# First block's sparse attention: DVE and ACT work in single-head pieces, the first decay level ahead of the scores, and a projection tile inside the last step

## What is computed

```python
# 1. sparse attention (NSA): 8 heads, 2 kinds of keys (selected, sliding), on top of compressed keys
p_slc = softmax(where(causal, q @ k_sel.T, NEG)); o_slc = p_slc @ v_sel
p_win = softmax(where(win_ok, q @ k_win.T, NEG)); o_win = p_win @ v_win
o     = g0 * o_cmp + g1 * o_slc + g2 * o_win
y_a   = o @ w_proj_nsa
# 2. gated linear attention (GLA): attn[t, s] = sum_d q[t,d] k[s,d] exp(b[t,d] - b[s,d]), s <= t
o     = attn @ v;  o = rms_norm(o) * g * silu(r)
y_b   = o @ w_proj_gla
# mixed = sigmoid(m_a) * y_a + sigmoid(m_b) * y_b;  h = h + mixed @ w_out
# 3. the second block's modulations, for both of its layers
mod   = silu(c) @ ada_w[l] + ada_b[l]
```

## Time and profile before

| | us |
|---|---|
| median of 3 runs (range) | 1208.77 (1208.45 to 1209.26) |
| the profiled execution | 1204.53 |
| its span in the profile | 1202.7 |
| the stage: first scores to the first projection | 137.80 to 216.45 of the span |
| PE busy over the span | 1088.9 (91%) |
| DVE, ACT, POOL busy | 470.7, 411.8, 206.4 |

### The profile page before, as it was taken

How to read it: one execution, slowest core, us unless ns; L and a number is a source line. 1 busy time by engine, 2 the same in 40 slices (tenths; PEclk the granted TensorE clock), 3 DMA queues, 4 the chain that set the end, 5 groups by cost and what they waited for, 6 DMA issues and landing times. The chain is left out here.

```text
span 1202.7 us, 17403 instructions
## 1 busy us (share of the span) xinstructions
PE 1088.9 (91%) x6862; PEld 706.4 (59%) x6862; DVE 470.7 (39%) x1037; ACT 411.8 (34%) x786; POOL 206.4 (17%) x277
## 2 busy tenths in 40 slices
PE   8999888899898889788989899979999899999997
PEld 7887555557432324344545235346887676999775
DVE  4565366445200000133332112107747546344654
ACT  5444353343101001014332102004436454444872
POOL 1005363000000000002120000004422223001550
PEclk9999899999999999999999999999999999999998
DMA  9657399745799999999999999995531203766300
GB/s 364 233 173 259 126 350 351 266 175 226 286 425 426 422 426 415 424 427 401 418 428 422 422 423 421 424 419 205 172 128 53 89 21 121 223 182 190 107 20 35
DMA packets 55720, 333.58 MB, mean 277 GB/s; under 512 B 5840, under 2 KB 6096, under 8 KB 43216
## 3 DMA queue, kind: packets, MB, share of 16 engines
q1 hardware_dynamic: 55632, 332.39, 71.1%
HBM read 331.32 MB, written 1.05 MB: 276 GB/s over the span
## 5 line engine op out<-in xcount | busy, mean ns | idle before, releaser
L486 ACT ACTIVATE ab<-w 128x1024 fp32r<-128x1024 f32 (+2 forms) x117 | 122.0, 1049 | 178.9 <-PE ps L502 170.2
L496 DVE TENSOR_TENSOR ab<-w,ab 128x1024 fp32r<-128x1024 f32 (+2 forms) x96 | 116.8, 1223 | 133.4 <-ACT ab L486 133.0
L2548 PE MATMUL ps<-w,vT 128*32 128x512 f32 x1024 | 129.1, 629 | 41.2 <-DMA w<-in_w_gate 28.2
L502 PE MATMUL ps<-ab,uA 128*128 128x512 f32 x320 | 102.5, 402 | 5.8 <-POOL ab L496 2.6
L2548 PEld LDWEIGHTS ps<-w,vT 128*32 128x32 f32 x1024 | 29.1, 111 | 121.8 <-issue 79.7
L502 PE MATMUL ps<-UA,ab 128*128 128x256 f32 x512 | 93.8, 284 | 2.8 <-ACT h L1573 1.5
L502 PE MATMUL ps<-ab,UA 128*128 128x512 f32 (+1 forms) x288 | 87.9, 386 | 0.6 <-POOL UB L624 0.6
L502 PEld LDWEIGHTS ps<-UA,ab 128*128 128x128 f32 x512 | 80.2, 192 | 3.5 <-issue 1.7
L2596 PE MATMUL ps<-w,bT 128*32 128x512 f32 x512 | 62.0, 608 | 16.5 <-DMA w<-in_w_down 10.9
L502 PEld LDWEIGHTS ps<-ab,uA 128*128 128x128 f32 x320 | 60.5, 192 | 20.8 <-issue 3.4
L496 POOL TENSOR_TENSOR ab<-w,ab 128x1024 fp32r<-128x1024 f32 (+1 forms) x21 | 49.9, 2380 | 132.7 <-DVE Am L1804 88.1
(11 more groups left out here) (547 smaller groups left out, 1858.7 us busy)
## 6 DMA issues: line engine op xcount, KB each, us to landing
w<-in_w_gate SPq DMA_DIRECT2D x32, 2048.0 KB, 13.3
w<-in_w_up SPq DMA_DIRECT2D x32, 2048.0 KB, 12.9
w<-in_w_down SPq DMA_DIRECT2D x32, 2048.0 KB, 13.2
w<-in_w_ada SPq DMA_DIRECT2D x48, 512.0 KB, 7.6
w<-in_w_c SPq DMA_DIRECT2D x42, 512.0 KB, 4.5
w<-in_w_m SPq DMA_DIRECT2D x16, 512.0 KB, 5.3
w<-in_ab_out_w SPq DMA_DIRECT2D x10, 512.0 KB, 4.4
w<-in_w_out SPq DMA_DIRECT2D x8, 512.0 KB, 9.8
```

What stands on the lines that cost most here:

```text
L486: e.activation(sp.a(j), w.v, ACT.Copy).then_inc(sp.whole, 1)
L496: e.tensor_tensor(sp.b(j), w.v, sp.a(j).bitcast(F32), ALU.subtract).then_inc(sp.parts[j % NAB], 1)
L502: ins = e.matmul(out_, l[x], r[y], start=start and n == 0, stop=stop and n == 2)
L2548: ins = e.matmul(t.ps[o, :], ve[:, p % 2, 2 * c + k, o], w.v[:, 2 * a + k, :], start=c + k == 0, stop=c + k == 4)
```

## The change

**1. Single-head pieces.** `masked`, `weighted` (DVE), `turned`, `weights` (ACT) now do one head per call, and the table places the two heads in slots of their own. In the same table `turned_out` goes from slot 8 to 6, `weighted` from slot 5 to 7 and 9, and POOL's `roots` from slot 0 to 2.

**2. First decay level ahead.** `DECAY_AHEAD = 3`: each engine takes three steps of its decay generator before the stage. For POOL these hold level 0's L1073, L1074 and L1083, L1084 (lines 1074, 1075, 1084, 1085 now); for ACT level 0's exponential, behind the second L1659 copy and before the output of `m01`; for PE and DVE nothing but the yields. So all later decay work is written six slots earlier against the attention and the modulations.

**3. A projection tile in the last step.** PE's table gets `(1, 2, behind)`, which for the last pair calls `project`: `pnsa0` of row tile 0 is computed between the last pair's `turn` and `out`, in a bank of `FIVE`, after the copies of the row tile 0 pairs alone. Row tile 1 follows in its old place.

```diff
+        DECAY_AHEAD = 3
...
-            return nsa_steps([(0, 2, turn), (0, 0, scores), (5, 2, out)])
+            def behind(p):
+                if p == len(NSA_PAIRS) - 1:
+                    last()
+
+            return nsa_steps([(0, 2, turn), (0, 0, scores), (1, 2, behind), (5, 2, out)])
...
-            return nsa_steps([(2, 0, masked), (5, 1, weighted), (8, 2, turned_out)])
+            return nsa_steps([(1, 0, lambda p: masked(p, 0)), (2, 0, lambda p: masked(p, 1)), (6, 2, turned_out),
+                              (7, 1, lambda p: weighted(p, 0)), (9, 1, lambda p: weighted(p, 1))])
...
-            return nsa_steps([(1, 2, turned), (3, 0, weights)])
+            return nsa_steps([(1, 2, lambda p: turned(p, 0)), (2, 2, lambda p: turned(p, 1)),
+                              (3, 0, lambda p: weights(p, 0)), (6, 0, lambda p: weights(p, 1))])
...
-            return nsa_steps([(0, 1, roots)])
+            return nsa_steps([(2, 1, roots)])
...
+            def project(n, x, p, c, i, ring=ALL):
+                ts, t = slice(i * 128, (i + 1) * 128), bank.take(ring, p + str(c))
+                free(e, t)
+                if c == 0:
+                    for y in bank[n] if n == "ogT" else bank[n][i::2]:
+                        e.wait_ge(y.evac, y.n)
+                for k in range(4):
...
+                    ins = e.matmul(t.ps[:, :], x[:, k, ts], w.v[:, k % 2, :], start=k == 0, stop=k == 3)
+                ins.then_inc(t.full, 1)
...
+            decayed = pe_decayed(e, TWO)
+            for _ in range(DECAY_AHEAD):
+                next(decayed)
+            rest = turns(pe_modulations(e, ONE), decayed)
+            beside(pe_nsa(e, FIVE, lambda: project("nsa_o", ynT, "pnsa", 0, 0, FIVE)), rest)
...
+            decayed = act_decayed(e)
+            for _ in range(DECAY_AHEAD):
+                next(decayed)
             act_lin(e, S1, "m01", [xsm[:, i, 0, :] for i in range(2)], more=0, scaled=True)
-            rest = turns(act_modulations(e), act_decayed(e))
+            rest = turns(act_modulations(e), decayed)
```

More of the change, by code:

```diff
@@ L1218, in nsa_steps, with pe_nsa @@
                     yield
-        def pe_nsa(e, ring):
+        def pe_nsa(e, ring, last):
             turned = {}
@@ L1298, in turned_out, with turned @@
                 e.tensor_copy(ynT[:, j, i * 128:(i + 1) * 128], t.ps[:, 0:128]).then_inc(t.evac, 1)
-            return nsa_steps([(2, 0, masked), (5, 1, weighted), (8, 2, turned_out)])
+            return nsa_steps([(1, 0, lambda p: masked(p, 0)), (2, 0, lambda p: masked(p, 1)), (6, 2, turned_out),
+                              (7, 1, lambda p: weighted(p, 0)), (9, 1, lambda p: weighted(p, 1))])
         def act_nsa(e):
-            def turned(p):
+            def turned(p, hp):
                 n = 256 * (NSA_PAIRS[p][1] + 1)
[L1305 to L1311, removed]
@@ L1313, in weights @@
-            def weights(p):
+                u, t = 2 * p + hp, bank["nsa_t"][2 * p + hp]
+                if u >= 3:
+                    g = bank["nsa_o"][(u - 3) // 2]
+                    e.wait_ge(g.full, g.n)
+                e.wait_ge(t.full, t.n)
+                e.activation(bT[:, u % 3, 0:n], t.ps[:, 0:n], ACT.Copy).then_inc(t.evac, 1)
+            def weights(p, hp):
                 i, m = NSA_PAIRS[p][1], st[:, p % 4, :]
                 n = 128 * (i + 1)
[L1316 to L1325, removed]
@@ L1327, in act_nsa @@
-            return nsa_steps([(1, 2, turned), (3, 0, weights)])
+                u, t = 2 * p + hp, bank["nsa_s"][2 * p + hp]
+                e.wait_ge(t.evac, t.n)
+                if u >= 4:
+                    g = bank["nsa_t"][u - 4]
+                    e.wait_ge(g.full, g.n)
+                for kind in range(2):
+                    o, c = slice(kind * n, kind * n + n), 2 * hp + kind
+                    ins = e.activation(NSA_P[u % 4][:, o], bS[:, hp, o], ACT.Exp, bias=m[:, c:c + 1], scale=-1.0, accum_out=m[:, 4 + c:5 + c])
@@ L1543, in pe_first @@
                     for i in range(2):
-                        ts, t = slice(i * 128, (i + 1) * 128), bank.take(ALL, p + str(c))
-                        free(e, t)
-                        if i == 0 and c == 0:
-                            for y in bank[n]:
-                                e.wait_ge(y.evac, y.n)
-                        for k in range(4):
-                            w = W[f"{p}{c}.{k // 2}"]
-                            if i == 0 and k % 2 == 0:
-                                e.wait_ge(w.full, w.n)
-                            ins = e.matmul(t.ps[:, :], x[:, k, ts], w.v[:, k % 2, :], start=k == 0, stop=k == 3)
-                        ins.then_inc(t.full, 1)
-                    for k in range(2):
-                        W.release(f"{p}{c}.{k}", t.full, t.n)
+                        if c + i > 0 or n == "ogT":
+                            project(n, x, p, c, i)
             pe_idle_next(e, ALL, 4)
@@ L1856, in dve_first @@
             dve_lin(e, S1, "m01", more=0)
-            rest = turns(dve_modulations(e), dve_decayed(e))
+            decayed = dve_decayed(e)
+            for _ in range(DECAY_AHEAD):
+                next(decayed)
+            rest = turns(dve_modulations(e), decayed)
             beside(dve_nsa(e), rest)
@@ L1926, in pool_first @@
                 e.tensor_tensor(st[:, 2 + i, :], st[:, 2 + i, :], gate[:, i, 0:24:3], ALU.mult).then_inc(c_rec, 1)
-            beside(pool_nsa(e), turns(idle_modulations(), pool_decayed(e)))
+            decayed = pool_decayed(e)
+            for _ in range(DECAY_AHEAD):
+                next(decayed)
+            beside(pool_nsa(e), turns(idle_modulations(), decayed))
             pool_rsqrt(e, 2, 2, (squared, 2))
```

41 lines of the change are left out of this document (22 added, 19 removed).

## The result

| | before | after |
|---|---|---|
| median (range), 22 runs each | 1209.42 (1204.26 to 1218.50) | 1214.45 (1209.92 to 1221.67) |
| ratio | | 1.0039, 95% interval 1.0024 to 1.0054 |
| the profiled execution, its span | 1204.53, 1202.7 | 1214.65, 1212.8 |
| first scores to the last transposes (L570) | 85.59 | 92.47 |
| PE busy / not busy in it | 72.44 / 13.15 | 77.07 / 15.40 |

What follows compares the result with a forecast made beforehand. PE's own work was taken to set the stage, leaving only its waits to win. Start -4.9, middle 0, end +5.8, behind +0.3, clock +3.2 sum to +4.4 us: 1213.2 us, 8 in 10 from 1205.5 to 1216.5.

Steps and rivals of the forecast that it cites:

- start: Start of the stage, up to pair 1's scores: 4.9 us less, 1.5 of them the clock.
- middle, waits: Pair 1's scores to `out` of pair 5: PE's waits 5.85 us against 5.89 before, so no change.
- (a): End of the stage: chunk 11 waits 2.8 us for DVE, which has other work ahead of chunk 10's sum.
- (d): Last `turn` (pair 7), head 0: waits 1.35 us while DVE copies pair 6 out, sums chunk 11 and scales.
- (e): Last `turn`, head 1: waits 3.05 us, its scaling standing behind the GLA's four closing products on DVE.
- clock behind them: Lower PE clock after the end's long waits: +3.2 us, chunk 11 losing 1.5 and project tile 0 1.7.
- behind it: After the stage: `pgla0`'s second tile waits for bank 4, shared with tile 0; +0.3 us.
- (c): End of the stage: `out` of pair 6 waits 0.6 us for `bT`, 0.46 before.
- That the middle's waits go: Rival, faster: smaller pieces make the middle's 5.9 us of waits vanish, 1204.1 us; chance 0.22.
- The loads: Rival, slower still: modulation loads set the middle's pace, costing 2.4 us there, 1215.6 us; chance 0.08.
- The clock's rival: Rival, no change: the clock holds without any drop, sum +1.2 us, 1210.0 us; chance 0.22.
- The shift: Rival, no change: something behind the stage is late anyway and the 4.4 us vanish there; chance 0.06.

Runs made afterwards that it cites:

- ahead: Part 2 alone against the kernel before: first decay level ahead, old table of whole pairs, no projection tile in the last step; 1207.00 us, ratio 0.9981.
- scale: The change, with DVE scaling the last pair's head 1 directly behind head 0, ahead of the closing products; 1208.81 us, ratio 1.0006 to the kernel before.
- idle: The change, with 4 idle matmuls ahead of chunk 11's products and 5 between the last turn's heads; 1209.58 us, ratio 1.0011 to the kernel before.
- project: Part 3 alone against the kernel before: projection tile in the last step, old table, no decay level ahead; 1208.21 us, ratio 0.9991.
- ahead_project: Parts 2 and 3 against the kernel before, on the old table of whole pairs; 1207.19 us, ratio 0.9974.
- pieces: Part 1 alone against the kernel before: new table by head, no decay level ahead, no projection tile in the last step; 1213.23 us, ratio 1.0037.
- sums: The change, with DVE's closing chain of the GLA (copy, squares, closing products) written behind all modulations; 1214.82 us, ratio 1.0049 to the kernel before.
- ahead_project_sums: Parts 2 and 3 on the old table, with DVE's closing chain written behind all modulations; 1213.91 us, ratio 1.0033 to the kernel before.
- both: The change with the edits of `scale` and `sums` together; 1213.03 us, ratio 1.0031 to the kernel before.

## Why the prediction was right, point by point

**Direction and size.** 1213.2 was forecast, +4.4 us on the median; measured 1214.45, +4.7 by the ratio. The terms, read in the profiled executions:

| step | forecast | profile | also shown by |
|---|---|---|---|
| start | -4.9 | -5.10 | `ahead`, all with part 2: 6.14 to 6.15 us |
| middle, waits | 0 (5.85 for 5.89) | +0.8 (6.65) | |
| middle, clock | 0 | +1.6 | not in `scale`, `idle` |
| end (a), chunk 11 | 2.8 | 2.47 | `scale`, `idle` |
| end (d), (e), last `turn` | 1.35, 3.05 | 1.37, 2.70 | `scale` removes (e) |
| end, waits in all | +5.8 (9.1 for 3.36) | 8.31 - 3.36 = +4.95 | |
| clock behind them | +3.2 (1.5 and 1.7) | +4.4 (1.6 and 2.7) | `idle`: about 3.4 |
| behind it | +0.3 | +0.4 (7.51 for 7.10) | `project` |

Within the table: the middle's waits were mis-sized at level 4 (0.67 for 0.1), level 7 (1.02 for 0.6) and chunk 6 (0.53 for 0.8); level 3's 1.52 for 1.5 and chunk 2's 1.29 for 1.25 held. The end's larger waits were a little shorter than worked out, (c) too (0.46 for 0.6). Tile 0 took 5.91 us for 5.2, and head 1's transposes ahead of it 1.09 for 0.66. Some sums are looser than they look: the pieces named for level 3 give 1.3 us and not 1.5, those for (a) of the end 2.7 and not 2.8.

The signs that were named came: pair 1's scores 6.14 us after the first at a grant of 1.00, the waits of DVE's sum and scaling in their places, tile 0 near half its rate, and 53.71 busy us in the middle, under the 55 that would have spoken against it. Only the end of the stage came later than named: it is 6.9 us longer in the profile, where the terms gave 4.1.

**Where it was luck.** That the sum comes within half a microsecond of the median is partly luck. In the profiled execution the same terms come to 7.3 us (6.88 and 0.4), and two of them were off by about 0.8 with opposite signs: the middle's waits too low, the end's too high. The 0 for the middle hides two effects of 3.0 and -2.0 us (see `scale`): the level ahead adds waits, and the pieces take part of them away. The working counted them together and gave neither a size.

**The term that was wrong** is the clock in the middle. The forecast took the lower grant to follow waits of about 3 us, and put none behind level 3's 1.5 us. In this execution it followed that wait too and cost 1.83 - 1.16 + 2.87 - 1.92 = 1.6 us. It followed this wait in three of eight profiled executions (below), so the median should hold less of it than this profile.

**The rivals.** That the middle's waits go was wrong: 6.65 us are left. The breaking-up advice behind that rival (the Trainium skill, "Perfetto Trace Analysis", section "Optimizing Scalar/DVE Operations") says only that it may help, and here it does so in one place: beside the level ahead, the pieces shorten PE's waits in the middle from 8.47 to 6.65 us (`ahead_project` and `scale`). On the whole they lose: `pieces` alone is 1.0037, since a piece that is written later in its engine's queue is late for a PE that was never waiting for it. The loads did not bind: PE's timeline of the stage has no wait for a load, and `scale` took the middle in 58.74 us with loads at 355 GB/s, while the experts' stretch again moved 422 GB/s, above the 358 GB/s that the Trainium skill, "DMA: Bandwidth & Descriptors", section "Where 436 GB/s comes from", gives for a core. The clock's rival was wrong in its size: idle work takes some 3.4 us back. The shift was not swallowed.

**What the forecast did not say** is which parts (e) comes from. It needs two parts: with the pieces alone the closing products are written six slots later and start behind head 1's scaling (217.50 and 215.63 in that kernel's trace), and with parts 2 and 3 both scalings, in slot 5, stand ahead of them (208.53 and 209.05, the products from 211.32 on). Only six slots earlier and by head do the products slip between the two heads. (The two parts without the third were not run; the third changes nothing in DVE's queue.) This is the interaction spoken of above, and `scale`, which undoes it alone, gets 4 us back.

**Still open.** Whether (a) can be removed without a new wait: `sums` only showed that moving the whole closing chain is wrong. A finer order, with chunk 10's sum ahead of the copy and square alone, was not tried.

## What to carry to other kernels

Before moving work earlier or in smaller pieces, write out the queue of each engine around the waits that matter. A piece is worth something only if somebody waits for it: here the pieces took some 2 us of waits out of the middle, and the piece that was not early enough at the end (a scaling behind four products, a sum behind a copy and a square) made PE wait. Parts that are good one by one must be tried together with the table that places them; here two of three parts gained 0.26% together and the third lost more than that. Where a wait can't be removed, idle matmuls that fit into it cost nothing that could be measured here and may keep the clock for what comes behind: worth a try where such waits precede long products.

## What the runs showed of the hardware

A wait of the same length in the same place is followed by the lower clock in one execution and not in another. Behind the wait of 1.52 to 1.58 us ahead of level 3, level and chunk took 4.7 us in the change, in `ahead` and in `ahead_project_sums`, and 3.1 us (1.16 and 1.92) in `scale`, `sums`, `both`, `idle` and `ahead_project`. Behind 2.47 us chunk 11 took 3.55 us in the change, and behind 2.48 us 1.92 in `scale`. In `pieces` a wait of 2.33 us was followed by a chunk of 1.92 us, while the 3.10 us of the kernel before and of `project` were each followed by a slow chunk (3.44 and 3.48 us). Longer waits were followed by a slow projection each time: 2.70 us (5.91), 4.66 and 2.09 (5.38), 5.12 (4.64), 3.89 and 1.21 (6.36, for 3.60 at the full clock). But in `pieces` the last transposes (1.09 us for 0.60), `out` (1.98 for 1.09, grant 0.50 from 218.31 to 220.22) and the projection (8.51 for 7.10) ran slow behind waits of only 1.30 and 0.41 us, while `scale` kept the full clock behind 1.37. So the length of the last wait alone does not decide. What does decide between two executions of the same wait, these runs don't show. So one profile can't price such a stretch: in the profiled executions the change's stage is 6.9 us longer, in the medians the kernel is about 5 us slower.
